# Hybrid decoder layer on eight cores: dependency ranges, the planner's key, the decode tile and the order of the first transfers

## What is computed

```python
h = x + 0.5 * rms_norm(swiglu(rms_norm(x, ng[0]), f1_gate, f1_up, f1_down), ng[1])
mix, s_new, conv_new = token_mixer(rms_norm(h, ng[2]), s0, conv0, w_in, w_gate_up, b_gate, gla_norm_g, conv_w, w_out)
h = h + rms_norm(mix, ng[3])
h = h + 0.5 * rms_norm(swiglu(rms_norm(h, ng[4]), f2_gate, f2_up, f2_down), ng[5])
gate = sigmoid(rms_norm(h, ng[6]) @ w_ple_gate)
h = h + rms_norm((p @ w_ple_proj) * gate, ng[7])
```

## Time and profile before

| | us |
|---|---|
| median of three runs | 1688.74 (1688.3 to 1689.0) |
| the profiled execution | 1689.24 |
| its span on the slowest core (core 0) | 1687.7 |
| spans of the other cores | 1681.4 to 1685.6 |

### The profile page before, as it was taken

One profiled execution on the slowest core, in us unless ns is written; L12 is line 12 of the kernel. 1 busy time (PEld: TensorE's weight loads), 2 busy tenths in 40 slices (PEclk: granted clock), 3 DMA queues, 4 the chain that ended last, 5 costly groups with the idle time before them and its releaser, 6 DMA issues.

```text
span 1687.7 us, 28373 instructions; the slowest of 8 cores (1681.4 to 1687.7 us)
## 1 busy us (share of the span) xinstructions
PE 1514.3 (90%) x9039; PEld 1446.8 (86%) x9039; DVE 830.3 (49%) x1825; ACT 707.2 (42%) x1375; POOL 286.7 (17%) x543
## 2 busy tenths in 40 slices
PE   5999989738999989999899899988999899899992
PEld 4999978527999879999798899978999798899982
DVE  2341367743431575423795442377431588443157
ACT  3112565505212753125665411574112766621273
POOL 2222112001222211221111122211222111122210
PEclk9999999758999989999999999998999999999996
DMA  9677547124777658776355577846877455477631
GB/s 292 191 207 212 185 123 214 33 69 127 210 206 208 193 178 251 207 207 202 113 150 163 147 205 210 244 146 181 233 208 210 126 158 154 127 209 207 202 123 67
DMA packets 86432, 299.47 MB, mean 177 GB/s; under 512 B 9728, under 2 KB 10512, under 8 KB 86288
## 3 DMA queue, kind: packets, MB, share of 16 engines
q0 software_dynamic: 77504, 278.20, 57.4%
q1 hardware_dynamic: 8784, 19.46, 3.7%
HBM read 286.87 MB, written 10.75 MB: 176 GB/s over the span
## 4 chain that ended last, share of the span: by engine, by line
PE 80%; DVE 9%; ACT 4%; issue 3%; DMA 3%; DVEq 0%; POOL 0%; ACTq 0%; SPq 0%; POOLq 0%
PE ps_bank L317 80%; DVE sb_h L356 2%; DMA sb_wslot<-ws 2%; DVE sb_hr L361 2%; DVE sb_xn L356 1%; ACT sb_tg L346 1%; ACT L346 1%; DVE sb_hr L356 1%; ACT sb_xn L351 1%; ACT sb_rb L346 1%; DMA gla_s<-sb_hr 1%; DVE sb_tg L356 1%; DVE sb_tg L361 1%; ACT sb_ef L346 0%; DVEq L196 0%
## 5 line engine op out<-in xcount | busy, mean ns | idle before, releaser
L317 PE MATMUL ps_bank<-sb_xn,sb_wslot 128*128 128x344 f32 x5568 | 961.5, 328 | 35.8 <-DVE sb_hr L361 12.1
L317 PEld LDWEIGHTS ps_bank<-sb_xn,sb_wslot 128*128 128x128 f32 x5568 | 909.1, 193 | 56.3 <-issue 53.2
L309 POOL DMA_DIRECT2D sb_wslot<-ws x522 | 277.5, 534 | 1245.7 <-PE ps_bank L317 1240.9
L317 PE MATMUL ps_bank<-sb_hr,sb_wslot 128*128 128x344 f32 x2592 | 448.1, 324 | 6.2 <-DVE sb_hr L356 4.9
L317 PEld LDWEIGHTS ps_bank<-sb_hr,sb_wslot 128*128 128x128 f32 x2592 | 420.8, 191 | 9.1 <-issue 8.4
L346 ACT ACTIVATE sb_tg<-sb_tg 128x344 f32<-128x344 f32 (+3 forms) x349 | 169.5, 494 | 466.2 <-DVE sb_tg L356 464.5
L356 DVE TENSOR_TENSOR sb_hr<-ps_bank,sb_tg 128x344 fp32r<-128x344 f32 x288 | 147.6, 516 | 212.9 <-PE ps_bank L317 197.0
L356 DVE TENSOR_TENSOR sb_tg<-ps_bank,sb_rn_0 128x344 f32<-128x344 f32 x264 | 135.5, 516 | 202.2 <-PE ps_bank L317 195.5
L356 DVE TENSOR_TENSOR sb_ef<-sb_ef,sb_tg 128x344 f32<-128x344 f32 x120 | 61.7, 514 | 192.5 <-ACT sb_tg L346 186.6
L317 PE MATMUL ps_bank<-sb_rb,sb_csr 128*128 128x344 f32 (+2 forms) x259 | 90.3, 381 | 60.1 <-ACT sb_rb L346 34.1
L346 ACT ACT_TABLE_LOAD x93 | 119.3, 1283 | 58.5 <-PE ps_bank L317 21.9
(11 more groups left out here) (80 smaller groups left out, 644.0 us busy)
## 6 DMA issues: line engine op xcount, KB each, us to landing
sb_wslot<-ws POOLq DMA_DIRECT2D x522, 512.0 KB, 4.7
sb_h<-x SPq DMA_DIRECT2D x24, 344.0 KB, 6.1
y<-sb_h SPq DMA_DIRECT2D x24, 344.0 KB, 3.8
sb_hr<-p POOLq DMA_DIRECT2D x6, 344.0 KB, 5.3
sb_hr<-sg POOLq DMA_DIRECT2D x8, 256.0 KB, 3.1
gla_s<-sb_hr SPq DMA_DIRECT2D x8, 256.0 KB, 2.0
sb_csr<-csr POOLq DMA_DIRECT2D x1, 192.0 KB, 7.1
sb_cst<-cst SPq DMA_DIRECT2D x1, 177.5 KB, 12.3
```

The costliest lines, as they stand in the source:

```text
L309: P.op(eng, lambda e: e.dma_start(out=dst_ap, in_=src_ap), reads=list(reads), writes=list(writes), dma=name, is_output=is_output, cost=dst ...
L317: ins = e.matmul(out.ap, a.ap, b.ap, start=st, stop=sp)
```

## The change

The decode tokens move to tile 2 (lane 0, pass 2). `sample_gla` is cut into generators: one for the 16 block matrices, now built on POOL, and one for each piece; the two matmuls of a piece add up in one bank (the k columns stand between zeros, which one more DVE operation writes), so that one add of 128 partitions replaces two. The wait for the convolution goes. `_reg_write` splits a partly covered record. The planner's key adds 1.28 us to an activation that needs another table, and ranks lanes by the blocks that are left to the end of the stage; its model of transfers has one shared pipe for all queues. `posts` issues a one-element `Ln` ahead of its last output. For lane 0 the next tile's squares are spawned within F2. The last tile's squares are summed by matmuls, and two of its eight tail columns go to POOL. In the opening the constants go first, on ACT's queue; `x` is spread over SP's and ACT's; the early weight blocks wait for given parts of `x`, and the rest follows. The diff, cut to its core:

```diff
-ST = 1
+ST = 2
...
     def _reg_write(self, w, tok):
         lst = self.recs.setdefault(w.base, [])
-        lst[:] = [rec for rec in lst if not (w.lo <= rec[0] and rec[1] <= w.hi)]
-        lst.append([w.lo, w.hi, tok, {}])
+        keep = []
+        for rec in lst:
+            if rec[1] <= w.lo or w.hi <= rec[0]:
+                keep.append(rec)
+                continue
+            if rec[0] < w.lo:
+                keep.append([rec[0], w.lo, rec[2], dict(rec[3])])
+            if w.hi < rec[1]:
+                keep.append([w.hi, rec[1], rec[2], dict(rec[3])])
+        keep.append([w.lo, w.hi, tok, {}])
+        lst[:] = keep
...
-            self.dma_t[eng] = max(self.dma_t[eng], t0) + cost
-            self.tdone[tok] = self.dma_t[eng] + 2000.0
+            self.dma_t = max(self.dma_t, t0 + 1500.0) + cost
+            self.tdone[tok] = self.dma_t + 500.0
...
         class ActOp(Op):
+            def swap(self):
+                return 1280.0 if acost(self.out, self.func)[1] != P.table else 0.0
...
         def posts(T, bks, g, half):
             for m in range(8):
+                if m == 7:
+                    yield act(scr.v(0, 1), eps, AF.Ln, extra=[eps], bias=eps.ap)
                 yield Hold(lambda: m in bks)
...
         def ffn(T, u0, gpost):
+            if u0 == U_F2 and T.lane == 0 and T.t + 2 < NT:
+                yield Hold(lambda: len(hok) == NJ)
+                spawn(nx(tiles[T.t + 2]), 4)
...
+                    yield dve(lambda e: e.tensor_scalar(out=kz4[:, :, 1, :], in0=cst.v(C_ONE, C_ONE + 128, 0, NS, a=2).ap, scalar1=0.0, scalar2=0.0, op0=ALU.mult, op1=ALU.add),
+                              [cst.v(C_ONE, C_ONE + 128)], [kz], 200.0)
...
                 yield Hold(lambda: all(st.get(s, 0) is None for s in range(nch)))
                 if T.sample:
-                    yield Hold(lambda: all(T.conv_done))
                     yield from sample_gla(T, E, OM, X_VS, X_S0, X_V, X_KM, X_QZ)
...
         def convs(bks):
...
+                if T.sample:
+                    dma("sp", "o_convs", convs_d[:, :], scs.v(0, 128).ap, reads=[scs.v(0, 128)], is_output=True)
...
         def sample_gla(T, E, OM, X_VS, X_S0, X_V, X_KM, X_QZ):
-            dma("sp", "o_convs", convs_d[:, :], scs.v(0, 128).ap, reads=[scs.v(0, 128)], is_output=True)
+            st = {"ld": 3, "vs": 0, "kv": 0, "o": 0, "end": 0}
             for pc in range(3):
                 load_s0(R, X_S0, pc)
             bo = yield Get("bank", 2)
-            for pc in range(8):
...
-                bs = yield Get("bank", 2)
-                for hh in range(2):
...
-                    yield dve((lambda o, i, d_: lambda e: e.tensor_tensor(out=o.ap, in0=i.ap.unsqueeze(1).to_broadcast([NS, 4, 128]), in1=d_.ap.unsqueeze(2).to_broadcast([NS, 4, 128]), op=ALU.mult))(vs, vi, idc),
-                              [vi, idc], [vs], 700.0)
-                for hh in range(2):
-                    yield mm(bs[hh].v(0, 512), [(R.v(X_KM + pp * 128, X_KM + (pp + 1) * 128, 0, NS, r=True), R.v(X_VS + hh * 512, X_VS + (hh + 1) * 512, 0, NS, r=True))])
-                    yield tt(S(p0, p0 + 64, r=True), S(p0, p0 + 64), bs[hh].v(0, 512, p0, p0 + 64), ALU.add)
+            def vsgen():
+                for i in range(16):
+                    yield Hold(lambda: st["kv"] >= i - 1)
...
+                    yield Op("pool", (lambda o, i_, d_: lambda e: e.tensor_tensor(out=o.ap, in0=i_.ap.unsqueeze(1).to_broadcast([NS, 4, 128]), in1=d_.ap.unsqueeze(2).to_broadcast([NS, 4, 128]), op=ALU.mult))(vs, vi, idc),
+                             [vi, idc], [vs], 1300.0)
+                    st["vs"] = i + 1
+            def piece(pc):
+                yield Hold(lambda: st["ld"] > pc)
+                yield dve(lambda e: e.tensor_tensor(out=S(a=4, r=True).ap, in0=S(a=4).ap, in1=ec.ap.unsqueeze(2).to_broadcast([128, 4, 128]), op=ALU.mult),
+                          [S(), ec], [S()], 700.0)
+                yield Hold(lambda: st["kv"] == 2 * pc)
+                bk, = yield Get("bank")
                 for hh in range(2):
+                    yield Hold(lambda: st["vs"] > 2 * pc + hh)
+                    yield mm(bk.v(0, 512), [(R.v(c0, c0 + 128, 0, NS, r=True), vsb[hh])], hh == 0, hh == 1)
+                    st["kv"] += 1
+                yield tt(S(r=True), S(), bk.v(0, 512), ALU.add)
...
                 if pc + 3 < 8:
+                    yield Hold(lambda: st["vs"] >= min(16, 2 * pc + 6))
                     load_s0(R, X_S0, pc + 3)
+            spawn(vsgen(), 1)
+            for pc in range(8):
+                spawn(piece(pc), 1)
+            yield Hold(lambda: st["end"] == 8)
...
         def ple(T):
             def sqs():
-                    yield from acc_sq(T, m, PR(m), 0.5)
+                    if T.t < NT - 1:
+                        yield from acc_sq(T, m, PR(m), 0.5)
+                        continue
+                    yield act(b_.v(0, W, r=True), PR(m), AF.Square, scale=0.5)
+                    if m in PTAIL:
+                        yield act_s(PR(m, True), PR(m), gcol(7, m, True))
+                    yield mm(by.v(0, W), [(onesD, b_.v(0, W, r=True))], first=(m == 0), last=(m == 7))
...
         def tail(T):
+            def on_pool():
+                for c in PTAIL:
+                    yield tt(PR(c, True), PR(c), q.v(0, W), ALU.mult, "pool")
+                    yield tt(T.hc(c), T.hc(c), PR(c), ALU.add, "pool")
+                    fin(c)
+            if last:
+                spawn(on_pool(), 0)
...
+            def rank(self):
+                if self.lane is None:
+                    return self.prio
+                b = self.item.blk
+                if b is None:
+                    return 8
+                return 8 + (min(e for e in (U_M // BU, U_F2 // BU, U_P // BU, BPP) if e > b % BPP) - b % BPP) / 1000 + self.lane / 1e6
...
-                        k = (g.item.start(), g.prio, g.n)
+                        k = (g.item.start() + g.item.swap(), g.rank(), g.n)
...
+        dma("act", "c_cst", cst.v(0, C_W).ap, cst_d[:, :], writes=[cst.v(0, C_W)])
         for c2 in range(4):
-            load_x(tiles[0], c2)
-        dma("sp", "c_cst", cst.v(0, C_W).ap, cst_d[:, :], writes=[cst.v(0, C_W)])
+            load_x(tiles[0], c2, "act" if c2 % 2 else "sp")
+        wissue()
+        wissue()
         dma("pool", "c_csr", csr.v(0, CR_W, r=True).ap, csr_d[:, :], writes=[csr.v(0, CR_W)])
-        for _ in range(NSLOT):
-            wissue()
         for c2 in range(4):
-            load_x(tiles[1], c2)
+            load_x(tiles[1], c2, "act" if c2 % 2 else "sp")
+        wissue([tiles[0].hc(5)])
+        wissue([tiles[0].hc(7)])
+        wissue([tiles[1].hc(1)])
+        wissue([tiles[1].hc(3)])
+        wissue([tiles[1].hc(7)])
...
+        while wi["issued"] < NSLOT:
+            wissue()
+        dma("sp", "scin", scs.v(0, 128).ap, sc_d[:, :], reads=[tiles[1].hc(7)], writes=[scs.v(0, 128)])
         for c2 in range(4):
             load_x(tiles[2], c2)
-        dma("sp", "scin", scs.v(0, 128).ap, sc_d[:, :], writes=[scs.v(0, 128)])
```

More of the change, by code:

```diff
@@ L382, in build_program, with wissue @@
         NB = NPASS * BPP
-        def wissue():
+        def wissue(after=()):
             g = wi["issued"]
@@ L528, in chain @@
             if src == "F":
-                yield tt(l_, by.v(0, W), T.ef.v(W, 2 * W), ALU.add)
+                yield tt(l_, by.v(0, W), T.ef.v(ep * W, (ep + 1) * W), ALU.add)
                 free("bank", by)
@@ L890, in sample_gla @@
             R, np_ = T.hr, T.np
-            dma("sp", "o_convs", convs_d[:, :], scs.v(0, 128).ap, reads=[scs.v(0, 128)], is_output=True)
+            vsb = [R.v(X_VS + i * 512, X_VS + (i + 1) * 512, 0, NS, r=True) for i in range(2)]
+            st = {"ld": 3, "vs": 0, "kv": 0, "o": 0, "end": 0}
             for pc in range(3):
@@ L894, in sample_gla @@
             bo = yield Get("bank", 2)
-            for pc in range(8):
[L896 to L901, removed]
-                bs = yield Get("bank", 2)
-                for hh in range(2):
-                    hd = 2 * pp + hh
+            def vsgen():
+                for i in range(16):
+                    hd, hh, g4 = 2 * (i // 8) + i % 2, i % 2, i // 2 % 4
+                    yield Hold(lambda: st["kv"] >= i - 1)
                     vs = R.v(X_VS + hh * 512, X_VS + (hh + 1) * 512, 0, NS, r=True, a=4)
@@ L982, in tail, with fin @@
             PR = lambda m, r=False: T.hr.v(HP_R + m * W, HP_R + (m + 1) * W, r=r)
-            by = yield from sq_mean(T)
+            last = T.t == NT - 1
+            if last:
+                yield Hold(lambda: isinstance(T.sq, Buf))
+                by = T.sq
+            else:
+                by = yield from sq_mean(T)
             q, = yield Get("tg")
             yield from rstd(by, W, q)
+            def on_pool():
[3 more added lines that the diff above has]
+                    fin(c)
+            fc = set()
+            def fin(c):
+                fc.add(c)
+                if c ^ 1 in fc:
```

(19 more changed lines are left out.)

47 lines of the change are left out of this document (34 added, 13 removed).

## The result

The kernel after takes **1631.65 us** (median; 1631.09 to 1631.79) against 1688.87 for the kernel before; the ratio on record is 0.9635, with an interval of 0.9555 to 0.9715.

A forecast was written before the change was run, and what follows sets the result against it. The prediction took PE as full between some 250 us of waits at known places. Terms 45 + 12 + 46 + 11 + 8 = 122 off 1689.2, less 0.5 to the median, gave 1567 us; range 1520 to 1635.

The forecast's parts named there:

- decode: Stage M: 65 us leave pass 1; 9 of matmuls and 10 bare come back in pass 2; 46 us gained.
- lane rank, in M: Stage M, three passes: ranking lanes by distance covers both lanes' chains, 15 of 28 us each, 45 us gained.
- P, both passes: Stage P, passes 1 and 2: 6 of 23 us lost come back each time, 12 us gained.
- opening: Start of the kernel: first weight matmul at 8 to 10 us, 14 us lost instead of 25, 11 us gained.
- end: Last tile: squares on PE 3 us, tail columns on POOL 2.5, lane rank some 2; 8 us gained.
- the 165 named as wrong: Stage M of pass 2: forecast near 150 us; a window above 165 would show the prediction wrong.
- The lag of 11 blocks on both sides: Stage M: lane 1 may go from 11 blocks behind to 11 ahead, 28 us of cover for the decode chain.
- the decode stays bare: Rival, 17%: in pass 2 lane 1 too stands at its output projection, 34 instead of 10 us bare; 1606 us.
- the round I put at 8.7 us: Decode: one buffer's load, decay, matmuls, add, store and two issues take 8.7 us; eight pieces in three buffers 23 us.
- Exact ranges, nothing on top: `load_x` records: 42 DVE waits, 25.3 us, go, counted within M's and P's terms; without cover 25 us at most.
- Table loads, zero: ACT's 93 table loads, 119 us: grouping some is worth zero while chains are covered, 23 us if not.
- DVE and POOL: Decode builds on POOL, 1.3 us each; rival, 10%: each holds up DVE, 21 us lost, 1588 us.

The follow-up runs named there:

- run 2: The changed kernel with the decode tokens' state update and outputs left out (call of `sample_gla` replaced by `pass`): 1593.24 us.
- run 12: The changed kernel with decode in lane 1, pass 1, old generators and old dependency records: 1638.6 to 1640.6 us on four cores of one die.
- (11): The changed kernel with decode in lane 1, pass 1, and the old generators (piece loop of before): die 0 at 1624.3 us.
- (8): The changed kernel with the decode tokens back in tile 1 (lane 1, pass 1), new generators kept: die 0 at 1613.1 us.
- run 1: The changed kernel with the old lane rank (lane 0 always first): 1648.78 us; by die 1637.9 and 1644.1.
- run 4: The changed kernel with all four stores of y issued before the four loads of the next x in the tail: 1621.49 us, 1617 by die.
- run 5: The changed kernel with the old dependency records and one range for `load_x`: 1665.91 us, die 0 at 1646.5.
- run 7: The changed kernel with `csr` first on POOL's queue and tile 1's `x` held behind tile 0's in the opening: die 0 at 1627.2 us.
- run 6: The changed kernel without the planner's 1.28 us for a table and without the early `Ln` in `posts`: die 0 at 1629.1 us.
- run 3: The changed kernel with the 16 block matrices built on DVE instead of POOL: 1633.7 us; by die 1629.8 and 1629.7.

## Why the prediction was right and wrong

The sum, term by term, from the windows above (P and the end by time lost or length, the decode as 65 gone from pass 1 less the 40 of run 2, M as what its windows shorten beside that: 11, 3 and 12):

| term | forecast, us | measured, us |
|---|---|---|
| decode | 46 | 25 |
| lane rank, in M | 45 | 26 |
| P, both passes | 12 | -6 |
| opening | 11 | 4 |
| end | 8 | 6 |
| sum | 122 | 55, of 57 in all |

By die the way from before to after is 1685, then 1639 to 1642 with all but the records, the generators and the move (12), 1624 with the records (11), 1613 with the generators (8), 1626 with the move: about -44, -17, -11, +13.

*Decode, 46 us: the step that failed.* "Lane 1 may meanwhile go ... 28 us ... 10 us stay bare": 30 did (run 2). M of pass 2 came to 183.3, not 150, 33 of the 65 us between forecast and result, and above the 165 named as wrong. The lag of 11 blocks on both sides, my reason against the rival "the decode stays bare", did not help. In the 50 us at half clock lane 1 gets 40 weight matmuls of its convolution in, 40 x 0.158 = 6 us of work, which stand between a piece's own matmuls; then it has its own attention to do, which ends when the decode does, and full-size matmuls go on only with the output projection, at 849.88. As far as these rows show, that is the condition of the rival, which had 17%, and its 34 us bare are near the 30. I priced the cover at full clock, and as if lane 1 had weight blocks left. The pace is a match by luck: the round I put at 8.7 us in three buffers, 2.9 a piece, is near the 3.1 of lane 1, but there PE's small matmuls and the wait for DVE's add, 2.17 + 0.94, make it up. I also took the old decode's 65 us as what its instructions cost. The row had the 13.3 us of waits in it, which I passed over; they belonged to the records (run 12), not to the code or the lane.

*Lane rank, 45 in M.* Right in kind: no stall over 4 us is left in front of lane 1's first M and F2 matmuls, as forecast. Passes 1 and 3 are 11 and 12 us shorter, 10 and 11 of it the rank's (run 1); I had 15. In pass 2, where the decode stands, it gives nothing.

*P, 12 us: none.* The sign was wrong. The stall of 5.54, behind DVE in lane 0's tail, was to shrink; it became 8.72, and 2.74 without the rank (run 1), so the rank that gained in M lost 5 to 6 us in each P. SP's queue, four round trips of store and load that were there before the change too, costs another 5 to 6 (run 4); the prediction does not mention it.

*Exact ranges, nothing on top.* Mis-sized: about 16 us in the decode of lane 1 (run 12), and the end's gain (run 5).

*End, 8: 6 to 7.* Right in size, but it hung on a term I put at nothing: with the new tail and old records, 41 us are lost as before (run 5), since the records make DVE's share of the tail wait for POOL's. Its three parts were not tried apart.

*Opening, 11: 4.* Less than the lower bound of 6 (on core 0, with 120 matmuls in 38.09 us, it is 6). The first weight matmul came at 13.12, not before 10, and waited for its weight block. I took 292 GB/s "throughout", which is the mean of 42 us; in the first 13.1 us after moves 221:

```profile
0.00:13.10 13.10, 0.00 (x0) 0.01 (x1) 2.86 (x12) 3.03 (x5) 2.50 (x8) 1.00 0.85 221
```

The 2.8 MB that I counted take 12.7 us at that rate, not 9.5. That the order of `x` was not the cause is shown (run 7); that the rate was is argued.

*Table loads, zero*: 3 us at most (run 6). *DVE and POOL*: builds of 1.14 us, forecast 1.3; the lock that the rival priced at 21 us shows as 3 us of DVE and costs nothing (run 3).

## What to carry to other kernels

Price work that is meant to cover a chain of small dependent steps at the clock which that stretch is granted, check that the other lane still has it by then, and ask what it does to the chain when it shares the in-order engine: here the same decode cost 13 us less where nothing stood between its pieces. A rule that helps one boundary should be read at all of them: the rank gained 10 us in M and lost 5 to 6 in P. Before a stage is rewritten, look up each long wait on a transfer in its rows: a planner's coarse records can invent it, and mending them (about 16 us) paid more than new code (11). A queue that alternates stores with loads into the same place makes a round trip of every pair: 23 us for four here, 10 with the stores first.

## What was not expected of the hardware

A granted clock of 0.50 over 50 us in which PE counts as 68 to 100% busy in every 10 us: the busy share at half clock hides the loss. A multiply-add on DVE of 569 ns lasts 954 beside GpSimd's builds, and the build of 16x512, 0.67 us on DVE, 1.14 on GpSimd, 1.7 times as long.
